# A Conformer's depthwise convolution on TensorE: 16 channels at 8 shifts, even and odd tokens in separate columns, in place of 32 channels at 4 shifts

## What is computed

```python
def conformer_conv(h, w_pw1, b_pw1, w_dw, b_dw, ln_g, ln_b, w_pw2, b_pw2):
    a, gate = jnp.split(h @ w_pw1 + b_pw1, 2, axis=-1)
    u = a * jax.nn.sigmoid(gate)
    dw = lax.conv_general_dilated(            # depthwise, 31 taps, causal
        u, w_dw[:, None, :], window_strides=(1,), padding=((CONV_WIDTH - 1, 0),),
        dimension_numbers=('NWC', 'WIO', 'NWC'), feature_group_count=D_MODEL) + b_dw
    ...                                       # layer norm of dw over the channels
    z = jax.nn.silu(z).astype(h.dtype)
    return z @ w_pw2 + b_pw2
```

## Time and profile before

| | |
|---|---|
| median of 3 runs | 1121.58 us (1121.51 to 1122.6) |
| the profiled execution | 1122.24 us |
| its span | 1120.4 us |
| TensorE matmul busy | 1114.8 us, 7338 instructions |
| VectorE busy | 836.6 us |
| ScalarE busy | 610.5 us |
| DMA moved | 203.53 MB, mean 182 GB/s |
| granted TensorE clock | 0.998 of full speed |

### The profile page before, as it was taken

The page is one execution under the profiler, slowest core; times in us unless marked ns, Lnnn a source line. Parts: engine busy times, 40 slices in busy tenths (PEclk is TensorE's granted clock), DMA queues, the critical chain, the costliest instruction groups (busy, mean ns, idle before and its releaser), DMA issues.

```text
span 1120.4 us, 18845 instructions
## 1 busy us (share of the span) xinstructions
PE 1114.8 (100%) x7338; PEld 995.0 (89%) x7338; DVE 836.6 (75%) x1288; ACT 610.5 (54%) x952; POOL 46.0 (4%) x67
## 2 busy tenths in 40 slices
PE   9999999999999999999999999999999999999998
PEld 9999888888877988888899998888888789888887
DVE  7977877766775878777658867877765888877753
ACT  5645565554541756555543455566554677655631
POOL 4130000000000000000000000000000210000000
PEclk9999999999999999999999999999999999999999
DMA  9545555555493445555644645555654325555552
GB/s 314 190 153 185 179 195 190 190 192 185 160 281 108 151 171 206 188 188 200 213 152 154 223 151 186 190 188 188 218 196 151 125 102 188 187 190 188 183 199 69
DMA packets 35368, 203.53 MB, mean 182 GB/s; under 512 B 4176, under 2 KB 10576, under 8 KB 11984
## 3 DMA queue, kind: packets, MB, share of 16 engines
q1 hardware_dynamic: 35136, 202.32, 51.8%
q10 hardware_dynamic: 144, 0.01, 0.0%
HBM read 200.09 MB, written 2.23 MB: 181 GB/s over the span
## 4 chain that ended last, share of the span: by engine, by line
PE 96%; DVE 2%; DMA 1%; ACT 0%; issue 0%; SPq 0%; DVEq 0%; ACTq 0%
PE banks L421 46%; PE banks L434 24%; PE banks L397 5%; PE banks L403 5%; PE banks L400 5%; PE banks L474 5%; PE banks L457 1%; PE banks L460 1%; PE banks L463 1%; DMA raw_t<-w 1%; PE banks L1611 1%; DVE lo_t L328 0%; PE banks L1597 0%; DVE lo_t L315 0%; DVE scr L1369 0%
## 5 line engine op out<-in xcount | busy, mean ns | idle before, releaser
L328 DVE TENSOR_TENSOR lo_t<-raw_t,hi_t 128x1024 fp32r<-128x1024 f32 x364 | 439.8, 1220 | 12.0 <-ACT hi_t L322 10.9
L322 ACT ACTIVATE hi_t<-raw_t 128x1024 fp32r<-128x1024 f32 x364 | 376.1, 1050 | 107.3 <-PE banks L434 39.1
L421 PE MATMUL banks<-x,hi_t 128*128 128x512 f32 x1536 | 363.4, 391 | 0.0
L421 PEld LDWEIGHTS banks<-x,hi_t 128*128 128x128 f32 x1536 | 284.1, 188 | 57.2 <-issue 0.8
L434 PEld LDWEIGHTS banks<-x,lo_t 128*128 128x128 f32 x1536 | 193.5, 191 | 5.4
L434 PE MATMUL banks<-x,lo_t 128*128 128x256 f32 x1536 | 195.8, 283 | 0.0
L421 PE MATMUL banks<-f,hi_t 128*128 128x512 f32 x704 | 164.1, 390 | 0.0
L421 PEld LDWEIGHTS banks<-f,hi_t 128*128 128x128 f32 x704 | 130.6, 188 | 26.1
L560 DVE TENSOR_TENSOR scr<-banks,scr 128x512 f32<-128x512 f32 x88 | 60.9, 692 | 82.0 <-ACT scr L628 81.3
L434 PEld LDWEIGHTS banks<-f,lo_t 128*128 128x128 f32 x704 | 87.6, 192 | 1.9
L434 PE MATMUL banks<-f,lo_t 128*128 128x256 f32 x704 | 88.2, 283 | 0.0
(11 more groups left out here) (199 smaller groups left out, 1121.3 us busy)
## 6 DMA issues: line engine op xcount, KB each, us to landing
raw_t<-w SPq DMA_DIRECT2D x182, 1024.0 KB, 4.9
scr<-shifts SPq DMA_DIRECT2D x32, 142.0 KB, 3.8
raw_t<-w SPq DMA_DIRECT2D x3, 512.0 KB, 9.5
shifts<-scr SPq DMA_DIRECT2D x8, 144.0 KB, 3.6
h<-xT SPq DMA_DIRECT2D x4, 256.0 KB, 6.9
out<-h SPq DMA_DIRECT2D x8, 128.0 KB, 4.1
cst<-consts SPq DMA_DIRECT2D x1, 816.0 KB, 13.0
raw_t<-w SPq DMA_DIRECT2D x2, 256.0 KB, 5.1
```

What stands on the lines that cost most here:

```text
L322: e.activation(hi_t[:, p % RING, :], raw_of(p), ACT.Copy).then_inc(s_hi, 1)
L328: e.tensor_tensor(lo_t[:, p % RING, :], raw_of(p), hi_t[:, p % RING, :].bitcast(F32), ALU.subtract).then_inc(s_lo, 1)
L421: m = e.matmul(halves(banks[:, to[j], :]), hi_t[:, slot, r * P:(r + 1) * P], parts[:, ks[j], :, :], start=ks[j] == 0 and not low_first, st ...
```

## The change

The stacks hold 16 channels at 8 shifts instead of 32 channels at 4. `glu` writes even tokens and odd tokens of a channel as two runs of 144, so that a shift of two tokens is a shift of one column. Partition 64 o + 16 k + c of a stack holds the tokens of parity o of channel c, shifted by k columns. A convolution matmul's 32 output columns are 16 channels of even and 16 of odd tokens, and it streams 128 token pairs instead of 256 tokens: 8 channel groups x 4 tap groups = 32 matmuls of 128 columns. In DRAM a channel's shifted groups lie side by side, so that a stack is loaded by two DMAs of 64 partitions, each partition as one run of 1148 elements.

The result has rows in another order, therefore ScalarE copies it out of PSUM (`conv_out`) and four matmuls with a 0/1 matrix of 64 columns bring it back (`pe_turn`). The columns of the first projection are permuted on the host to suit. The stationary operands come from a 16-column identity and a table `convs` (128x656, one more load at the start; `cols` loses 256 columns and `consts` 32). Six of the eight are made in the first FFN. Stacks have six places, in the part of `f2` that is idle here. Convolutions 2 and 3 move behind projection 7, and the sums for the shift behind projection 6.

```diff
@@ sync_program
+            e.dma_start(cv[:, :], convs).then_inc(s_cv, 16)
@@ dve_ffn
+                if f == 0 and 4 <= u < 4 + NE:
+                    dve_diagonals(e, u - 4)
@@ sizes
-        US_C, SW, NU = 288, 284, 3
+        US_C, SW, NU = 288, 144, 3
+        ROW = 8 * SW
+        NE, NS = 6, 6
-        CONV_BANKS, STAT_BANK, NORM_BANKS = (3, 2), 6, (7, 0)
+        CONV_BANKS, STAT_BANK, NORM_BANKS = (3, 2, 5, 4, 3, 2, 5, 4), 6, (7, 0)
@@ store_unit, load_stack
-            e.dma_start(shifts[u], u_r[u % NU]).then_inc(s_kept, 16)
+            kept = bass.AP(shifts, u * P * US_C, [[SW, P], [P * SW, 2], [1, SW]])
+            e.dma_start(kept, u_r[u % NU].rearrange("p (o t) -> p o t", o=2)).then_inc(s_kept, 16)
-            for j in range(4):
-                again = bass.AP(shifts, u * P * US_C + j, [[US_C, 32], [32 * US_C, 4], [1, SW]])
-                e.dma_start(stack[u % NS][32 * j:32 * j + 32, :, :], again).then_inc(s_stack[u % NS], 16)
+            for o in range(2):
+                again = bass.AP(shifts, u * P * US_C + o * P * SW, [[1, 4], [ROW, 16], [1, ROW - 4]])
+                flat = stack[u % NS][64 * o:64 * o + 64, :, :].rearrange("p g t -> p (g t)")
+                e.dma_start(flat[:, 0:ROW - 4], again).then_inc(s_stack[u % NS], 16)
@@ pe_conformer
                 if u == 5:
+                    pe_turn(e, 0)
+                    pe_turn(e, 1)
+                if u == 6:
                     e.wait_ge(s_dw, 2)
...
-                if u == 6:
-                    pe_conv(e, 2)
-                    e.wait_ge(s_shift, 1)
-                    pe_conv(e, 3)
-            for u in range(4, KD):
+            pe_conv(e, 2)
+            for u in range(3, KD - 1):
                 pe_conv(e, u)
+                pe_turn(e, u - 1)
+            pe_conv(e, KD - 1)
             ps = banks[:, STAT_BANK, :]
-            e.wait_ge(s_sums, 2)
+            pe_turn(e, KD - 2)
+            e.wait_ge(s_sumd, 5)
+            e.wait_ge(s_sumq, 5)
             pe_stat(e, ps[:, 0:2], sum_d, True, False)
             pe_stat(e, ps[:, 2:4], sum_q, False, False)
-            e.wait_ge(s_dw, KD)
-            pe_stat(e, ps[:, 0:2], dw[:, 7, :], False, True)
-            e.wait_ge(s_csq, 7)
-            pe_stat(e, ps[:, 2:4], dsq[:, 7 % NQ, :], False, True).then_inc(s_cstat, 1)
+            pe_turn(e, KD - 1)
+            for u in (KD - 2, KD - 1):
+                e.wait_ge(s_dw, u + 1)
+                pe_stat(e, ps[:, 0:2], dw[:, u, :], False, u == KD - 1)
+                e.wait_ge(s_csq, u)
+                m = pe_stat(e, ps[:, 2:4], dsq[:, u % NQ, :], False, u == KD - 1)
+            m.then_inc(s_cstat, 1)
@@ pe_conv, pe_turn
-            for m in range(8):
-                for g in range(4):
-                    out_g = banks[32 * g:32 * g + 32, CONV_BANKS[u % 2], 0:T]
-                    last = plain(e, out_g, diags[u % NS][:, g, m, :], stack[u % NS][:, g, 4 * m:4 * m + T], m == 0, m == 7)
+            for r in range(2):
+                for m in range(4):
+                    for q in range(4):
+                        out_q = banks[32 * q:32 * q + 32, CONV_BANKS[u], r * P:(r + 1) * P]
+                        c = 32 * (4 * (4 * r + q) + m)
+                        last = plain(e, out_q, diags[u % NE][:, c:c + 32], stack[u % NS][:, 4 * r + q, 4 * m:4 * m + P], m == 0, m == 3)
+        def pe_turn(e, u):
+            e.wait_ge(s_crow, u + 1)
+            for odd in range(2):
+                turn = cv[:, V_TURN + 64 * odd:V_TURN + 64 * odd + 64]
+                for r in range(2):
+                    m = plain(e, banks[64 * r:64 * r + 64, CONV_BANKS[u], odd * P:(odd + 1) * P], turn, crows[u % 2][:, r * P:(r + 1) * P])
+            m.then_inc(s_turned_c, 1)
@@ act_conformer
+            def conv_out(u):
+                e.wait_ge(s_conv, u + 1)
+                if u >= 2:
+                    e.wait_ge(s_turned_c, u - 1)
+                e.activation(crows[u % 2], banks[:, CONV_BANKS[u], 0:T], ACT.Copy).then_inc(s_crow, 1)
+                if u == 4:
+                    conv_out(0)
+                    conv_out(1)
+            conv_out(2)
+            conv_out(3)
+            squares(0, 2)
             hi_to(e, G_PW2)
+            conv_out(4)
+            squares(2, 1)
+            conv_out(5)
...
@@ dve_conformer
-                e.scalar_tensor_tensor(u_r[u % NU][:, 30:30 + T], ct_r[u % 2][:, 0:T], colv("b_pw1", u), cs_r[u % 2],
+                to = u_r[u % NU].rearrange("p (o j) -> p o j", o=2)[:, :, 15:15 + T // 2]
+                e.scalar_tensor_tensor(to, by_token(ct_r[u % 2][:, 0:T]), colv("b_pw1", u), by_token(cs_r[u % 2]),
                                        ALU.add, ALU.mult).then_inc(s_cu, 1)
...
-                ps = banks[:, CONV_BANKS[u % 2], 0:T]
-                e.wait_ge(s_conv, u + 1)
+                ps = banks[:, CONV_BANKS[u], 0:T].rearrange("p (o j) -> p j o", o=2)
+                to = dw[:, u, :].rearrange("p (j o) -> p j o", o=2)
+                e.wait_ge(s_turned_c, u + 1)
```

More of the change, by code:

```diff
@@ L24 @@
 RING = 6
-SCR = 12288
+SCR = 12190
 EARLY = 4
@@ L188, in mark, with model_kernel @@
         return self.n
-def model_kernel(nc, w, poolw, xT, pos, cols, rows, consts, shifts, out):
+def model_kernel(nc, w, poolw, xT, pos, cols, rows, consts, convs, shifts, out):
     ctx = ExitStack()
@@ L1086, in model_kernel @@
         C3 = C2 + (NQ + 1) * T
[L1087 to L1091, removed]
+        NE, NS = 6, 6
+        idle = f2[:, KD:KF, :, :].rearrange("p a b c -> p (a b c)").bitcast(F32)
+        stack = [idle[:, n * 8 * SW:(n + 1) * 8 * SW].rearrange("p (g t) -> p g t", g=8) for n in range(NS)]
+        diags = [scratch(C3 + n * PIECE, PIECE) for n in range(NE)]
+        assert C3 + NE * PIECE <= SCR and NS * 8 * SW <= (KF - KD) * 2 * T
+        crows = [sq[:, n, :] for n in range(2)]
         cb = pw[:, :, :].rearrange("p a b -> p (a b)")
         shift, sum_d = ssum2[:, :], rb2[:, :]
-        mask = cst[:, C_MASK:C_MASK + 32]
         CPAIRS = (0, 6, 4)
-        CONV_BANKS, STAT_BANK, NORM_BANKS = (3, 2), 6, (7, 0)
+        CONV_BANKS, STAT_BANK, NORM_BANKS = (3, 2, 5, 4, 3, 2, 5, 4), 6, (7, 0)
         s_cpad, s_cside, s_cup, s_cscaled, s_sig = sem("cpad"), sem("cside"), sem("cup"), sem("cscaled"), sem("sig")
@@ L1220, in act_conformer @@
                                  bias=colv("b_pw1", 8 + v)).then_inc(s_sig, 1)
-                if u == 5:
-                    squares(0, 2)
+                if u == 4:
+                    conv_out(0)
+                    conv_out(1)
                 if u == 6:
                     hi_to(e, c + 11)
-                    squares(2, 1)
-                    squares(3, 1)
+            conv_out(2)
+            conv_out(3)
+            squares(0, 2)
             hi_to(e, G_PW2)
-            for u in range(4, KD):
-                squares(u, 1)
+            conv_out(4)
+            squares(2, 1)
+            conv_out(5)
+            squares(3, 1)
+            squares(4, 1)
+            conv_out(6)
+            squares(5, 1)
+            conv_out(7)
+            squares(6, 1)
+            squares(7, 1)
             e.activation(cs_r[0][:, 0:1], cs_r[0][:, 0:1], ACT.Silu)
@@ L1283, in take, with gather_d @@
                 else:
-                    e.scalar_tensor_tensor(dw[:, u, :], ps, colv("b_dw", u), shift, ALU.add, ALU.subtract).then_inc(s_dw, 1)
-            def gather(u, at, last=False):
+                    by = shift.rearrange("p (j o) -> p j o", o=2)
+                    e.scalar_tensor_tensor(to, ps, colv("b_dw", u), by, ALU.add, ALU.subtract).then_inc(s_dw, 1)
+            def gather_d(u):
                 e.wait_ge(s_dw, u + 1)
-                n = [e.tensor_tensor(sum_d, sum_d, dw[:, u, :], ALU.add)]
-                e.wait_ge(s_csq, at)
-                n.append(e.tensor_tensor(sum_q, sum_q, dsq[:, u % NQ, :], ALU.add))
-                for m in n:
-                    m.then_inc(s_sums if last else s_run, 1)
+                e.wait_ge(s_sumd, u - 1)
+                e.tensor_tensor(sum_d, sum_d, dw[:, u, :], ALU.add).then_inc(s_sumd, 1)
@@ L1295, in dve_conformer, with gather_q @@
+            def gather_q(u):
+                e.wait_ge(s_csq, u)
+                e.wait_ge(s_sumq, u - 1)
+                e.tensor_tensor(sum_q, sum_q, dsq[:, u % NQ, :], ALU.add).then_inc(s_sumq, 1)
             lo_to(e, G_PW1 + 16)
@@ L1298, in dve_conformer @@
             dve_dg(e, 2)
-            diagonals(0)
             lo_to(e, G_PW1 + 32)
@@ L1304, in dve_conformer @@
             scale(1)
-            diagonals(1)
             glu(0)
@@ L1328, in dve_conformer @@
                     e.wait_ge(s_cen, 1)
-                    e.tensor_tensor(sum_d, dw[:, 0, :], dw[:, 1, :], ALU.add).then_inc(s_run, 1)
-                if u == 6:
-                    e.wait_ge(s_csq, 1)
-                    e.tensor_tensor(sum_q, dsq[:, 0, :], dsq[:, 1, :], ALU.add).then_inc(s_run, 1)
-                    take(2)
-                    diagonals(5)
-                    take(3)
```

(35 more changed lines are left out.)

64 lines of the change are left out of this document (39 added, 25 removed).

## The result

The changed kernel took 1150.33 us (median of 4 runs, 1149.5 to 1152.42) beside 1122.09 for the kernel before (the three runs of the table above and one of 1123.68): 1.0254 times as long, 95% interval 1.0242 to 1.0266. The profiled execution took 1149.5 us, its span 1147.7. Faster was predicted, 1113.9. In this kernel the projection's matmuls are L426 and L439, all small ones L479, the split's high half L327, stack loads L1139 and st L1409.

What follows compares the result with a forecast made beforehand. TensorE was taken to bound the Conformer stage. Passes -13.6, turns +3.5, shape changes +1.2 and stage end +0.9 gave -8.0 us, so 1113.9 us from a median of 1121.58; 8-in-10 range 1111.5 to 1118.5.

Steps and rivals of the forecast that it cites:

- Two us to spare: I take nothing: DMA queue in the Conformer stage: last stack lands at 344.2, convolution 7 comes at 346.2; cost nothing, bounds 0 to +3 us.
- rival 1: Conformer stage: stack data come late, convolution 6 or 7 waits about 3 us; -5, 1117.2 by the profile; chance 0.20.
- The sum of the matmuls: TensorE in the Conformer stage: passes, turns, shape changes and stage end together give -8.0 us.
- Passes of half the width: Convolutions on TensorE: a round of four column tiles falls from 0.2165 to 0.110 us, -13.6 us over 128 rounds.
- rival 2: Convolutions: rounds don't shrink, bound by instruction delivery or by a fixed price per load and matmul; +5.6, 1127 us; chance 0.10.
- Turn and changes of shape: TensorE in the Conformer stage: turn matmuls cost +3.5 us, 11 more changes of tile shape at 0.11 each +1.2 us.
- The end of the stage: After the last convolution pass: take(7) and its square on VectorE lie open, +0.9 us (0.4 to 1.4).
- Diagonals in the first FFN: Six of eight diagonals move to VectorE in the first FFN, units 4 to 9, which just keeps pace; cost nothing.
- Strided glu and take: Conformer stage: strided glu and take lie under convolutions of 1.8 us each, except take(7); cost nothing.
- The constants at the start: Load of `convs`, 336 KB more at the start: some 0.5 us of transfer, costed at nothing (up to +0.5).
- theory K: From a follow-up experiment, TensorE's stops: an instruction packet comes late only while transfers of data are under way.

Runs made afterwards that it cites:

- channels-first version: The changed kernel with each stack load listing 16 channels outermost and the 4 shifts inside (taps and mask permuted to suit): 1119.49 us, 0.998 of the kernel before.

## Why the prediction was wrong

**The step that failed** is the one on the DMA queue: "Two us to spare: I take nothing", with 0 to +3 us as bounds, where idle time and half clock came to 33.8 us (below). It counted bytes at 305 GB/s and the time to issue, and set down as a point in favour "a row is one run of 4.6 KB". Neither helped here, because four engines carried the load. The diff had the answer in it, `[[1, 4], [ROW, 16], ...]` for `[[US_C, 32], ...]`; I read the length of the runs and not the order of the dimensions. With a DMA share of 0.27 they moved it at some 100 GB/s, a quarter of what weights got at the start (390) and a third of the 305. The order alone was worth 1150.33 - 1119.49 = 30.8 us.

**Why so much more than rival 1's 3 us.** Rival 1 had the right wait with the wrong price. The five gaps sum to 24.6 us. Each left a convolution at half clock: four at 3.64 and one at 3.28 make 17.8 us, where 5 x 1.96 is 9.8, so 8.0 more, and the three turns behind them (the first 1.12 in place of 0.66) 1.2. Against them stands the gain of the matmuls: 24.6 + 8.0 + 1.2 - 7.75 (below) = 26.1, and 0.7 for the later start of the first FFN, make 26.8 of the measured 27.45 at st. I had priced a stall as its length alone; here the clock added more than a third (9.2 us to 24.6).

**The sum of the matmuls held.** The run without the last two loads shows the stage as the prediction meant it. st starts at 352.35, its start of the first FFN 0.13 later than before (98.85 to 98.72): 7.75 us gained, against -8.0. The medians say 1121.81 - 1115.33 = 6.5: all four runs of this version have a mean clock of 0.998, like the profiled run of the kernel before, while of the seven runs of the kernel before in that series six have 1.0.

- *Passes of half the width.* Two convolutions take 338.33 - 334.70 = 3.63 us with one change of shape; less 0.11, 0.110 a round: as priced. Over 512 passes at a stretch (14.29 - 0.28) / 127 rounds = 0.110 again. So rival 2 is out, by either road.
- *Turn and changes of shape.* A turn with its two changes is 0.58 us, priced 0.44 + 0.22. A change is then worth 0.07 rather than 0.11.
- *The end of the stage.* Priced +0.9, and the size is right by luck. From the end of the convolutions to st went 1.99 us before, 4.14 without the last loads, of which 1.18 are two turns: 0.97 more. But take(7) and its square don't lie open. They run from 350.49 to 351.43, and TensorE has no idle time there. It has 24 statistics passes where 16 stood, because the sums now end at unit 5 and unit 6 has passes of its own; these eight at some 0.11 us are the 0.9.
- *Queue, once the loads use all engines.* Rival 1's place was right: stack 7, through the store that stands behind a chunk. The prediction gave this store 1.8 us to land; in the channels-first version it took 6.06, and 2.95 once the chunk stood elsewhere. It cost 1 us and went with that chunk's place.
- *Diagonals in the first FFN.* From the first FFN to the Conformer's first matmul lie 283.09 - 98.72 = 184.37 us before, 283.75 - 99.39 = 184.36 after. Nothing, as said. *Strided glu and take* cost nothing either: take lasts 0.48 us as before, and without the last loads TensorE has no idle time from 283 us to st.
- *The constants at the start.* Said to cost at most 0.5. The first FFN starts 0.67 us later than before, and moving them changed nothing (99.20 for 99.26), so it isn't their load.

**What the sum left out** even with good loads is the stop of 1.2 to 2.3 us, and the time at half clock, which differs from run to run: 1115.33 where there is no stop, medians of 1116.08 to 1119.49 where there is one. The prediction asked whether the sequencer delivers a load and its pass each 0.0275 us and answered from the array. It does, 512 of each in 14.29 us. That it stops at times is what no term had.

## What to carry to other kernels

Read a DMA's access pattern from the outside in. In these runs the outermost number on the DRAM side decided how many engines carried a load (share 0.27 at four, 0.44 at eight, 1.01 at sixteen, this one beside other loads), whatever its bytes and the length of its runs, and though 32 to 128 partitions stood on the other side. A share far below 1 while somebody waits for that queue is the sign in the profile. When a change halves the columns of a pass, it doubles the instructions for each us of TensorE: look for idle time that no semaphore explains, and price every stall together with the clock behind it.

## What was not expected of the hardware

- A load of 287 KB with four outermost lands so late that it also holds up what is queued behind it: chunks (ScalarE's longest wait 11.6 us, before 3.8) and stores (6.9 us to land, before 3.6).
- TensorE can stop for 1.2 to 2.3 us with no wait in its program, near the end of a packet of 16,384 bytes on the instruction queue, where passes of 128 columns run densely and loads of data are under way. What makes one packet late and its neighbour not is open: the same TensorE program stopped in convolution 4, in turn 4 or in convolution 7 as the loads around it moved, and no experiment separates theory K from a rival.
- In these runs the granted clock after a stall doesn't follow from the stall's length alone. It was 0.50 during or behind idle times of 3.37 and 3.41 us and behind all five of the changed kernel (3.45 us and more), but 1.00 behind one of 3.85 us. Of the stops, some had a stretch at 0.50 within 3 us behind them; the two in the half-width version of the kernel before had none at all.
